# Forgetting attention: GpSimd makes the keys' high parts and the second copies of the queries' high parts; VectorE's low parts of the keys move one step on

## The reference, cut to what matters

```
c = jnp.cumsum(lf_all, axis=1)                        # logarithms of the forget gates, per head
s = jnp.einsum('bqhd,bkhd->bhqk', q_blk, k_all) * scale
bias = cq[..., None] - c_k
s = jnp.where(mask, s + bias, -jnp.inf)               # causal
p = jax.nn.softmax(s, axis=-1)
o = jnp.einsum('bhqk,bkhd->bqhd', p, v_all)
```

## Time and profile before

| | |
|---|---|
| median of 3 runs | 1681.5 us |
| profiled execution | 1680.76 us |
| its span, first to last instruction | 1679.0 us |
| PE busy | 1651.5 us, 98% of the span |
| DVE busy | 1083.5 us, 65% |
| ACT busy | 775.8 us, 46% |
| POOL busy | 310.2 us, 18% |
| chain of work that ended last | PE 80%, DVE 9%, ACT 4%, issue 4%, POOL 2% |
| PE clock | 9 tenths or more in all 40 slices |

### The profile page before, as it was taken

The page is one execution under the profiler, slowest core; times in us unless marked ns, Lnnn a source line. Parts: engine busy times, 40 slices in busy tenths (PEclk is TensorE's granted clock), DMA queues, the critical chain, the costliest instruction groups (busy, mean ns, idle before and its releaser), DMA issues.

```text
span 1679.0 us, 27411 instructions
## 1 busy us (share of the span) xinstructions
PE 1651.5 (98%) x9540; PEld 1489.3 (89%) x9540; DVE 1083.5 (65%) x2322; ACT 775.8 (46%) x1630; POOL 310.2 (18%) x438
## 2 busy tenths in 40 slices
PE   8999999999999999999999999999999999999998
PEld 8999999999999988989988899888888888888886
DVE  7556666553999744454445597888877667774744
ACT  6477777765777533352233333222222334443521
POOL 1311111115333211124532230000000000000242
PEclk9999999999999999999999999999999999999999
DMA  5221212231222554563443422444432763444641
GB/s 187 77 61 41 79 47 59 67 110 36 74 57 67 163 179 160 160 210 123 147 140 111 134 85 94 131 144 144 144 131 105 258 220 111 132 149 125 192 163 75
DMA packets 164314, 205.34 MB, mean 122 GB/s; under 512 B 16152, under 2 KB 113240, under 8 KB 164208
## 3 DMA queue, kind: packets, MB, share of 16 engines
q1 hardware_dynamic: 164208, 203.97, 38.0%
HBM read 144.85 MB, written 57.28 MB: 120 GB/s over the span
## 4 chain that ended last, share of the span: by engine, by line
PE 80%; DVE 9%; ACT 4%; issue 4%; POOL 2%; DMA 0%; DVEq 0%; ACTq 0%; SPq 0%; POOLq 0%
PE gb L503 8%; PE gb L3173 6%; PE gb L2290 5%; PE sc L3173 5%; PE gb L2825 4%; PE gb L2661 4%; PE sc L2825 4%; PE tp L3173 4%; PE tp L2825 4%; PE tp L798 3%; PE sc L2449 3%; PE tp L2449 3%; PE gb L930 3%; PE gb L931 2%; PE gb L932 2%
## 5 line engine op out<-in xcount | busy, mean ns | idle before, releaser
L930 PE MATMUL gb<-Xh,wh 128*128 128x384 f32 (+1 forms) x504 | 175.9, 349 | 0.0
L489 POOL TENSOR_TENSOR wl<-raw,wh 128x256 fp32r<-128x256 f32 x168 | 125.0, 775 | 264.2 <-ACT wh L474 175.4
L931 PE MATMUL gb<-Xh,wl 128*128 128x384 f32 (+1 forms) x504 | 170.7, 339 | 0.0
L932 PE MATMUL gb<-Xl,wh 128*128 128x384 f32 (+1 forms) x504 | 170.7, 339 | 0.0
L3297 POOL TENSOR_TENSOR wl<-raw,wh 128x1024 fp32r<-128x1024 f32 x2 | 5.3, 2626 | 559.0 <-ACT wh L3288 559.0
L503 PE MATMUL gb<-Xh,wh 128*128 128x384 f32 (+1 forms) x288 | 103.9, 361 | 0.0
L503 PE MATMUL gb<-Xh,wl 128*128 128x384 f32 (+1 forms) x288 | 97.4, 338 | 0.0
L503 PE MATMUL gb<-Xl,wh 128*128 128x384 f32 (+1 forms) x288 | 97.3, 338 | 0.0
L930 PEld LDWEIGHTS gb<-Xh,wh 128*128 128x128 f32 x504 | 95.0, 189 | 0.1
L931 PEld LDWEIGHTS gb<-Xh,wl 128*128 128x128 f32 x504 | 95.0, 188 | 0.0
L932 PEld LDWEIGHTS gb<-Xl,wh 128*128 128x128 f32 x504 | 94.8, 188 | 0.0
(11 more groups left out here) (548 smaller groups left out, 4777.4 us busy)
## 6 DMA issues: line engine op xcount, KB each, us to landing
zr<-u_scr SPq DMA_DIRECT2D x91, 256.0 KB, 3.0
raw<-in_w_in SPq DMA_DIRECT2D x70, 256.0 KB, 3.2
u_scr<-ustore SPq DMA_DIRECT2D x26, 576.0 KB, 3.6
u_scr<-ustore SPq DMA_DIRECT2D x13, 768.0 KB, 3.2
sig_scr<-sig SPq DMA_DIRECT2D x16, 576.0 KB, 3.1
raw<-in_w_up SPq DMA_DIRECT2D x36, 256.0 KB, 4.4
kc<-in_cache_fox_k SPq DMA_DIRECT2D x8, 1024.0 KB, 5.6
vc<-in_cache_fox_v SPq DMA_DIRECT2D x8, 1024.0 KB, 7.6
```

Of the source, the lines that this page charges most:

```text
L489: nc.gpsimd.tensor_tensor(wl[U.slot][:, q], raw[U.slot][:, q], wh[U.slot][:, q].bitcast(F32), ALU.subtract).then_inc(w_lo if x == 3 else w ...
L930: nc.tensor.matmul(gb[c][:, 0:x1 - x0], wh[U.slot][:, ws], Xh3[:, k, x0:x1], start=(k == 0), stop=False)
L931: nc.tensor.matmul(gb[c][:, 0:x1 - x0], wl[U.slot][:, ws], Xh3[:, k, x0:x1], start=False, stop=False)
L932: last = nc.tensor.matmul(gb[c][:, 0:x1 - x0], wh[U.slot][:, ws], Xl3[:, k, x0:x1], start=False, stop=(k == KT - 1))
```

## The change

POOL takes over the copy of the next head's keys (step 8H-3, behind its zeroing) and the second copy of a query group (step 4M-2); the first copy of the queries stays on ACT. Head 0's keys and both copies of group 0 stay where they were. DVE's subtraction for the keys moves from step 8H-3 to step 8H-2, where it stands behind the subtraction for the queries and ahead of the output half and the inverse. Two semaphores, `q_two` and `k_two`, count POOL's copies; the waits on `q_hi` and `k_hi` get other numbers. The core of the diff:

```diff
+        def q_split_pool(pool, M):
+
+            q_free(pool, M)
+            q_half(nc.gpsimd.tensor_copy, M, 1).then_inc(q_two, 1)
...
+        def k_split_pool(pool, H):
+
+            hp = slice(DH * (H % 2), DH * (H % 2) + DH)
+            if H >= 2:
+                pool.wait_ge(sc_full, FOX_CH[8 * H - 8])
+            unit_kept(pool, u_k(H // 2))
+            nc.gpsimd.tensor_copy(kk[H % 2][hp, 0:KEYS], nB[hp, 0:KEYS]).then_inc(k_two, 1)
+
         def k_split_dve(v, H):
...
-            v.wait_ge(k_hi, H + 1)
+            if H:
+                v.wait_ge(k_two, H)
+            else:
+                v.wait_ge(k_hi, 1)
...
             if n % 4 == 0:
-                pe.wait_ge(q_hi, 2 * M + 2)
+                pe.wait_ge(q_hi, M + 2)
+                if M:
+                    pe.wait_ge(q_two, M)
...
                 if s < ITEMS:
                     fox_exp_act(act, s)
-                if s % 8 == 5 and (s + 3) // 8 < 8:
-                    k_split_act(act, (s + 3) // 8)
...
-                if s % 4 in (1, 2) and (s + 3) // 4 < 16:
-                    q_split_act(act, (s + 3) // 4, s % 4 - 1)
+                if s % 4 == 1 and (s + 3) // 4 < 16:
+                    q_split_act(act, (s + 3) // 4)
...
                 if s % 4 == 2 and M < 16:
                     q_split_dve(v, M)
-                if s % 8 == 5 and (s + 3) // 8 < 8:
-                    k_split_dve(v, (s + 3) // 8)
+                if s % 8 == 6 and (s + 2) // 8 < 8:
+                    k_split_dve(v, (s + 2) // 8)
                 if s >= 4 and s % 2 == 0:
                     fox_out_dve(v, s // 2 - 2)
...
                 if s < ITEMS:
                     fox_tail_pool(pool, s)
+                if s % 8 == 5 and (s + 3) // 8 < 8:
+                    pool.wait_ge(tail_zero, s + 1)
+                    k_split_pool(pool, (s + 3) // 8)
+                    pool.wait_ge(k_two, (s + 3) // 8)
+                if s % 4 == 2 and (s + 2) // 4 < 16:
+                    pool.wait_ge(tail_zero, s + 1)
+                    q_split_pool(pool, (s + 2) // 4)
+                    pool.wait_ge(q_two, (s + 2) // 4)
```

More of the change, by code:

```diff
@@ L403, in layer @@
         bf_in, lf_low, f_zero = sem("bf_in"), sem("lf_low"), sem("f_zero")
-        sq_done, xs_done, x_hi, x_lo = sem("sq_done"), sem("xs_done"), sem("x_hi"), sem("x_lo")
+        sq_done, xs_done, x_hi = sem("sq_done"), sem("xs_done"), sem("x_hi")
         lf_chain, lf_act, lf_done, cum_out = sem("lf_chain"), sem("lf_act"), sem("lf_done"), sem("cum_out")
@@ L410, in layer @@
         q_hi, q_lo, k_hi, k_lo, vs_done = sem("q_hi"), sem("q_lo"), sem("k_hi"), sem("k_lo"), sem("vs_done")
+        q_two, k_two = sem("q_two"), sem("k_two")
         kv_out, tab_in = sem("kv_out"), sem("tab_in")
@@ L415, in layer @@
         sink_set = sem("sink_set")
-        sig_done, sig_out = sem("sig_done"), sem("sig_out")
+        sig_out = sem("sig_out")
         rope_sh, rope_mv, rope_a, rope_b = sem("rope_sh"), sem("rope_mv"), sem("rope_a"), sem("rope_b")
@@ L945, in q_keep @@
                 act.wait_ge(q_kept, p - 1)
-                act.wait_ge(q_hi, 8 * (p - 1))
+                act.wait_ge(q_hi, 4 * (p - 1) + 1)
+                act.wait_ge(q_two, 4 * (p - 1) - 1)
                 act.wait_ge(q_lo, 4 * (p - 1))
@@ L957, in k_keep @@
                 v.wait_ge(k_kept, p)
-                v.wait_ge(k_hi, 2 * p)
+                v.wait_ge(k_hi, 1)
+                v.wait_ge(k_two, 2 * p - 1)
                 v.wait_ge(tp_full, K_ROUND[p - 1][-1] + 1)
@@ L976, in vb_keep @@
                 v.wait_ge(q_kept, 4)
-                v.wait_ge(q_hi, 32)
+                v.wait_ge(q_hi, Q_FOX)
+                v.wait_ge(q_two, 15)
             gemm_wait(v, Unit(U_VB), c)
@@ L1049, in rope_pool, with q_free, q_half, q_split_act @@
             nc.gpsimd.tensor_tensor(dst[:, a:b], dst[:, a:b], sh[:, 0:b - a], ALU.add).then_inc(rope_b, 1)
-        def q_split_act(act, M, y):
+        Q_FOX = 17
+        def q_free(eng, M):
+            if M >= 2:
+                eng.wait_ge(sc_full, FOX_CH[4 * M - 4])
+            unit_kept(eng, u_q(M // 4))
+        def q_half(copy, M, y):
             p, h, c0 = M // 4, M % 4 // 2, META + 512 * (M % 2)
[L1058 to L1061, removed]
             x = DH * (h ^ y)
-            nc.scalar.activation(qs[M % 2][x:x + DH, 0:512], nA[p % 2][DH * h:DH * h + DH, c0:c0 + 512],
-                                 ACT.Copy).then_inc(q_hi, 1)
+            return copy(qs[M % 2][x:x + DH, 0:512], nA[p % 2][DH * h:DH * h + DH, c0:c0 + 512])
+        def q_split_act(act, M):
+            copy = lambda to, src: nc.scalar.activation(to, src, ACT.Copy)
+            q_free(act, M)
+            q_half(copy, M, 0).then_inc(q_hi, 1)
+            if M == 0:
+                q_half(copy, M, 1).then_inc(q_hi, 1)
+        def q_split_pool(pool, M):
+            q_free(pool, M)
+            q_half(nc.gpsimd.tensor_copy, M, 1).then_inc(q_two, 1)
         def q_split_dve(v, M):
@@ L1069, in q_split_dve @@
             hp = slice(DH * h, DH * h + DH)
-            v.wait_ge(q_hi, 2 * M + 1)
+            v.wait_ge(q_hi, M + 2 if M else 1)
             nc.vector.tensor_tensor(qs[M % 2][hp, 512:1024], nA[p % 2][hp, c0:c0 + 512],
@@ L1080, in k_split_act @@
             hp = slice(DH * (H % 2), DH * (H % 2) + DH)
-            if H >= 2:
-                act.wait_ge(sc_full, FOX_CH[8 * H - 8])
             unit_kept(act, u_k(H // 2))
             nc.scalar.activation(kk[H % 2][hp, 0:KEYS], nB[hp, 0:KEYS], ACT.Copy).then_inc(k_hi, 1)
+        def k_split_pool(pool, H):
[4 more added lines that the diff above has]
+            nc.gpsimd.tensor_copy(kk[H % 2][hp, 0:KEYS], nB[hp, 0:KEYS]).then_inc(k_two, 1)
         def k_split_dve(v, H):
@@ L1380, in fox_dve @@
                 if s % 4 == 2 and M < 16:
-                    v.wait_ge(q_hi, 2 * M + 1)
+                    v.wait_ge(q_hi, M + 2)
                     q_zero_dve(v, M, DH - DH * (M // 2 % 2))
@@ L1537, in pre_dve @@
                 gp, lp = slice(DH * g, DH * g + DH), slice(DH - DH * g, P - DH * g)
-                v.wait_ge(k_hi, 8 + 2 * g + 2)
+                v.wait_ge(k_hi, 1 + 2 * g + 2)
                 nc.vector.tensor_tensor(kk3[g][lp, :, META:MB], keys_of(gp), kk3[g][gp, :, META:MB].bitcast(F32),
@@ L1609, in qb_split_dve @@
             hp, gp = slice(DH * h, DH * h + DH), slice(DH * (u_ // 2), DH * (u_ // 2) + DH)
-            v.wait_ge(q_hi, 32 + 4 * M + 2 * h + 1)
+            v.wait_ge(q_hi, Q_FOX + 4 * M + 2 * h + 1)
             if h == 0 and M % 8 < 2:
@@ L1625, in swa_scores_pe @@
             if n % 4 < 2:
-                pe.wait_ge(q_hi, 32 + 4 * M + 2 + 2 * h)
+                pe.wait_ge(q_hi, Q_FOX + 4 * M + 2 + 2 * h)
                 pe.wait_ge(q_lo, 16 + 2 * M + 1 + h)
@@ L1866, in swa_sp @@
                     sp.wait_ge(rope_b, 15)
-                    sp.wait_ge(q_hi, 32 + 4 * 15 + 4)
+                    sp.wait_ge(q_hi, Q_FOX + 4 * 15 + 4)
                     sp.wait_ge(q_lo, 16 + 2 * 15 + 2)
@@ L3512, in _ @@
             lf_act_(act)
-            for y in range(2):
-                q_split_act(act, 0, y)
+            q_split_act(act, 0)
             for n in (4, 5):
```

## The result

The changed kernel takes 1686.92 us (median of 7 runs, 1685.87 to 1688.69) against 1681.27 us of before in the same runs (7, 1680.36 to 1682.11): 5.65 us or 0.36% slower, ratio 1.0036 with a 95% interval of 1.0027 to 1.0046. Its profiled execution has a span of 1685.4 us, 6.4 us more than before.

A forecast was written before the change was run, and what follows sets the result against it. PE's own work was taken to bound the forgetting-attention stage (busy 300.4 of 305 us). Terms 3.7 + 4.1 - 0.2 = 7.6 us on 1680.76 us gave 1688.4 us, median forecast 1689.0 us; 8-in-10 range 1683.5 to 1693 us.

The forecast's parts named there:

- Rival 1: Delay of DVE and ACT in steps 6 to 8 absorbed, only steps 14, 30, 46 lose: 1685.0 us, chance 0.12.
- rivals 2 and 3: 2: ACT's relief shortens PE's waits, 1679.2 us, chance 0.08; 3: gains and losses lie beside PE, 1681.5 us, chance 0.08.
- rival 4: POOL's second query copy falls on DVE's step 8H-2 subtractions seven times: 4.9 us more, 1694 us, chance 0.08.
- The first kind: Steps 14, 30, 46: DVE has no gap, so the whole 1.24 us subtraction adds to PE's third-piece wait, 3.7 us.
- The relief of step 8H-3: DVE loses the subtraction and its waiting there, some 2.6 us a time; claimed to be worth nothing.
- The second kind: Steps 6, 22, 38, 54: later inverse, scaling, exponential and eviction delay PE in step 8 by 1.02 us, 4.1 us together.
- The gain of 0.2 us at the key rounds: Steps 5, 21, 37, 53: without ACT's key copy ahead, the eviction starts 0.06 us earlier, four times, 0.2 us.
- The sum: 3.7 + 4.1 - 0.2 = 7.6 us more on PE over the whole stage.
- the signs in the profile: Third-piece waits near 1.7 us in steps 15, 31, 47, small in 7, 23, 39, 55; about 1.1 us in step 8.
- VectorE and GpSimd in each other's way: If POOL's copy met DVE's subtractions, each meeting would add up to a copy's length.

The follow-up runs named there:

- e1: The changed kernel with DVE's subtraction for the keys put back to step 8H-3, POOL keeping its copies: 1680.53 us against 1680.65 us of before, ratio 0.9999.
- e2: The kernel before with only DVE's subtraction for the keys moved from step 8H-3 to step 8H-2, all copies staying on ACT: ratio 1.0038 to before.
- f4: The changed kernel with the subtraction moved back to step 8H-3 in steps 13, 29 and 45 alone: ratio 1.0022 to before.
- g1: g2 and f1 together: 1676.4 us against 1680.69 us of before, ratio 0.9974.
- g2: The kernel before with PE's key round put ahead of one fill portion in steps 5 and 6 of each pair of heads: ratio 0.9999 to before.
- f1: e1 with the zeros of qs in step 4M-2 made by POOL as well: 1678.65 us against 1680.81 us of before, ratio 0.9988.
- e3: The changed kernel with the subtraction in step 8H-2 put behind the inverse: ratio 1.0059 to before.

## Why the prediction was right, and where its sizes were off

- *The sign and the cause: right, and shown.* All of the loss is the place of VectorE's subtraction (e1 without it: 0.9999; e2 with it alone: 1.0038). Nothing of GpSimd's part costs anything that shows. Rival 1 (absorbed in steps 6 to 8) falls with f4, rivals 2 and 3 with the result, and rival 4 with the trace: the copies took 1.05 and 0.61 us (I had taken 1.3 and 0.7 us), in steps 5 and 6 at 91.26 and 96.48 us, and none met a subtraction of keys or queries; that of the keys took 1.236 us over the eight of them as before.
- *The first kind, 3 x 1.24 = 3.7 us: 3 x 1.15 = 3.4 us for the subtraction, and 3.0 us against before.* The mechanism held to the step: wait 1.62 instead of 0.48 us. The term was too large because I charged the row's duration. On the engine the next operation starts 1.16 us behind the subtraction (138.80 to 139.96 us above), since rows overlap by 0.08 us.
- *The relief of step 8H-3, put at nothing: 0.15 us, three times.* The prediction says that VectorE's work in step 14 begins when PE's scores arrive, "so that nothing earlier makes up for it". It missed the link over ScalarE: VectorE's low parts of the turned blocks waited 0.15 us for ScalarE, which was late through the inverse behind the old subtraction. Moving the copy (e1) or the subtraction (e2) ends that. So a loss of 1.15 us is 1.00 us net.
- *The second kind, 4 x 1.02 = 4.1 us: 3.1 us.* The path held link by link: subtraction, inverse (103.37 against 103.35 us as forecast), scaling (103.55 against 103.60), exponential (105.88 against 106.04), eviction (107.03 against 107.29), all in the time of before. The largest part of the 0.26 us lies between scaling and exponential: 2.33 us where I had taken 2.44 us. Behind 0.22 us of idle time ScalarE's rows don't overlap; with no idle time between them they do, by about 0.1 us. The rest is the eviction, 1.15 instead of 1.25 us behind the exponential's start.
- *The gain of 0.2 us at the key rounds: none in steps 5, 21 and 37, and at most 0.1 us behind step 53* (by e1's masking products). The 0.4 us that e1 gains are the 0.15 us above. That ScalarE's relief is worth nothing at the key rounds was right in this order of PE's work; g1 beside g2 and f1 shows that it is worth some 2 us once the key round stands one portion earlier.
- *The sum* was 7.6 us; the stage lost 6.1 us, 3.0 of the first kind and 3.1 of the second, and the median 5.65 us.
- *Of the signs in the profile,* the waits at the third piece came (1.62 us for "near 1.7"), and VectorE waits no more for the high parts of the seven. The others were smaller than forecast: no PE row at the third piece of steps 7, 23, 39 and 55 shows a wait, the row in step 8 shows 0.21 us instead of "about 1.1", and PE idles 9.4 us in the window instead of some 12. The time is lost all the same, 0.75 us each time; matmul rows reach into the wait, so that their idle time shows only part of it.
- *VectorE and GpSimd in each other's way* stayed out of it, as the second query copies lie some 4 us ahead of the subtractions, and the key copies further. No run here makes a copy meet one of these subtractions, so what that would cost stays open. Other meetings show that it depends on who comes first and on what GpSimd does. Its zeroing falls inside the moved subtraction (at 102.14 us in the changed kernel), and neither is longer for it (0.19 and 1.24 us). And ahead of the stage, head 0's subtraction meets one of GpSimd's that starts 0.05 us later:

```profile
63.67 1.23 DVE L1091 TENSOR_TENSOR kk<-nB,kk 64x1040 fp32r<-64x1040 f32 x1 [1.22 <-ACT kk L1084]
63.72 1.78 POOL L489 TENSOR_TENSOR wl<-raw,wh 128x256 fp32r<-128x256 f32 x1
```

VectorE's takes its usual time; GpSimd's takes 1.78 us, where the mean in the changed kernel's stage is 0.76 us. Behind the stage it goes both ways: VectorE's subtraction at 399.29 us, ahead of GpSimd's, takes 1.22 us, and that at 401.28 us, 0.21 us behind the start of one of GpSimd's, the 1.65 us of the earlier trace rows. Each time the one that came later paid.

## What to carry to other kernels

Work taken from an engine that waits wins next to nothing by itself (here 0.4 us of stage for 17 us taken off ScalarE), and a step that waited for its input may still be in the best place: here VectorE's 1.4 us of waiting lay in a stretch in which it had to wait for PE anyway, while a step later its list was the one that PE waited for. Before moving an operation, find in the timeline whether the first wait of that engine behind the new place is for the bottleneck (here the move was then free but for 0.15 us) or whether the bottleneck waits for it (here all of it counted), and follow the third engine too: ScalarE carried both the loss of steps 6 to 8 and the 0.15 us. Price a moved operation by the distance between starts, not by its row, and a wait of PE by its starts, not by the idle time shown.

## What the runs showed of the hardware that was not expected

- A single wait of PE of 1.87 us, in a stream of otherwise dense matmuls, was followed, 1.3 us after its end, by 3.4 us at the lower of its two clocks (granted 0.50), at a cost of 1.5 us; a wait of 1.62 us at the same place was not. It happened at each of the three places of e3. So 0.25 us more of waiting went with 1.75 us more of loss.
- GpSimd's copies into fp32r took no longer than ScalarE's: 0.606 us for 64x512, which goes into the other 64 rows, and 1.049 us for 64x1040, which stays in its rows, against 0.626 and 1.065 us.
